# A two-block mixer kernel: scores between gate quarters, PSUM banks of the decays, an output gate by seven half-block products

## The reference

```
z = h @ w_in                      # 512 tokens, and 256 context tokens before them
# first mixer (gated linear attention), 4 heads in 2 pairs, 2 directions, chunks of 64:
dec = exp(where(causal, b[t] - b[s], -inf))            # b: sums of log decays
att = einsum('bhtd,bhsd,bhtsd->bhts', q, k, dec)       # the "scores"
o   = (q * exp(b)) @ S + att @ v                       # S: running state
S   = S * exp(b_last) + (k * exp(b_last - b)).T @ v
# second mixer (gated delta rule): a 3x3 convolution per channel over a grid of 8 x 64
qkv = silu(conv_grid(concat(bq, bk, bv), gdn_conv))    # 1536 channels
bq, bk = l2norm(bq) * 128 ** -0.5, l2norm(bk)
# ... the chunked delta rule ...
ya = rmsnorm(oa) * silu(ag)       # ag = h @ w_in[:, AG], 512 columns
yb = rmsnorm(ob) * silu(bg)       # bg = h @ w_in[:, BG], 512 columns: the output gate
```

## Time and profile before

| | |
|---|---|
| median of 3 runs | 1341.34 us (1338.7 to 1341.41) |
| profiled execution | 1342.3 us, its span 1340.5 us |
| mean granted TensorE clock | 0.995 of full |
| PE, PEld busy | 1291.7 us (96%), 795.4 us (59%) |
| DVE, ACT, POOL busy | 694.0 us (52%), 413.0 us (31%), 396.9 us (30%) |

### The profile page before, as it was taken

The page is one execution under the profiler, slowest core; times in us unless marked ns, Lnnn a source line. Parts: engine busy times, 40 slices in busy tenths (PEclk is TensorE's granted clock), DMA queues, the critical chain, the costliest instruction groups (busy, mean ns, idle before and its releaser), DMA issues.

```text
span 1340.5 us, 23888 instructions
## 1 busy us (share of the span) xinstructions
PE 1291.7 (96%) x9603; PEld 795.4 (59%) x9603; DVE 694.0 (52%) x1422; ACT 413.0 (31%) x897; POOL 396.9 (30%) x470
## 2 busy tenths in 40 slices
PE   5999999999999999999999999998999999998997
PEld 3554655555666777778445786445655786445653
DVE  4366657846333434464465374237736383337735
ACT  4244303362432222201014102236623202236721
POOL 0100000211324443154530250127731150127731
PEclk9999899999999999999999999999999999999999
DMA  9710112101310100031254415110002515100001
GB/s 315 269 63 27 39 64 78 62 1 64 119 73 3 65 2 3 3 126 64 87 192 95 133 32 188 64 52 1 2 16 67 153 41 188 63 1 2 1 1 63
DMA packets 71533, 96.54 MB, mean 72 GB/s; under 512 B 27640, under 2 KB 35248, under 8 KB 71423
## 3 DMA queue, kind: packets, MB, share of 16 engines
q1 hardware_dynamic: 71050, 94.76, 21.1%
q10 hardware_dynamic: 372, 0.27, 0.1%
HBM read 92.89 MB, written 2.13 MB: 71 GB/s over the span
## 4 chain that ended last, share of the span: by engine, by line
PE 89%; DVE 4%; POOL 2%; ACT 2%; issue 1%; DMA 1%; ACTq 0%; SPq 0%; POOLq 0%; DVEq 0%
PE PS L147 85%; PE PS L2785 2%; DVE AR L2891 1%; ACT AR L3013 1%; POOL AR L3072 1%; DMA AR<-in_onehot 1%; DMA AR<-in_final_g 1%; POOL AR L2008 1%; PE PS L353 0%; POOL AR L3070 0%; DVE AR L2878 0%; ACT AR L3023 0%; PE PS L2119 0%; DVE AR L2061 0%; PE PS L1395 0%
## 5 line engine op out<-in xcount | busy, mean ns | idle before, releaser
L147 PE MATMUL PS<-AR 64*64 64x64 f32 (+14 forms) x8966 | 1218.8, 332 | 22.4 <-ACT AR L3023 6.5
L147 PEld LDWEIGHTS PS<-AR 128*128 128x128 f32 (+4 forms) x8966 | 725.4, 155 | 488.2 <-issue 392.0
L3013 ACT ACTIVATE AR<-AR 128x257 f32<-128x257 f32 (+5 forms) x160 | 84.9, 531 | 98.4 <-DVE AR L2891 89.0
L2891 DVE CUSTOM_DVE_ANT_0 AR<-PS,AR 128x257 f32<-128x257 f32 (+5 forms) x160 | 72.3, 452 | 60.7 <-PE PS L147 43.1
L412 POOL TENSOR_TENSOR AR<-AR 128x1 f32<-128x1 f32 (+4 forms) x26 | 21.9, 843 | 260.4 <-DVE AR L407 213.7
L1183 DVE SCALAR_TENSOR_TENSOR AR<-AR 128x441 f32<-128x441 f32 (+2 forms) x96 | 78.6, 819 | 15.7 <-ACT AR L1140 12.0
L1570 DVE TENSOR_TENSOR AR<-PS,AR 128x256 f32<-128x256 f32 x60 | 25.5, 425 | 100.7 <-PE PS L147 97.6
L3072 POOL TENSOR_SCALAR AR<-AR 128x257 f32<-128x257 f32 (+5 forms) x96 | 53.8, 560 | 58.5 <-DVE AR L2897 51.0
L3070 POOL TENSOR_SCALAR AR<-AR 128x128 f32<-128x128 f32 (+3 forms) x64 | 39.2, 613 | 63.1 <-DVE AR L2897 58.2
L1697 ACT ACTIVATE AR<-PS 128x512 f32<-128x512 f32 x48 | 28.7, 597 | 92.5 <-PE PS L147 90.1
L2008 POOL TENSOR_TENSOR AR<-AR 128x512 f32<-128x512 f32 x36 | 47.7, 1326 | 28.2 <-DMA AR<-in_w_o 25.2
(11 more groups left out here) (264 smaller groups left out, 941.8 us busy)
## 6 DMA issues: line engine op xcount, KB each, us to landing
AR<-in_w_in SPq DMA_DIRECT2D x16, 2048.0 KB, 8.9
AR<-in_w_mod SPq DMA_DIRECT2D x6, 2048.0 KB, 12.7
AR<-in_w_out SPq DMA_DIRECT2D x4, 2048.0 KB, 12.6
AR<-in_x SPq DMA_DIRECT2D x8, 512.0 KB, 5.6
AR<-in_w_in SPq DMA_DIRECT2D x4, 1024.0 KB, 7.4
AR<-in_w_o SPq DMA_DIRECT2D x2, 2048.0 KB, 7.8
AR<-in_w_in SPq DMA_DIRECT2D x2, 1664.0 KB, 8.7
AR<-in_w_in SPq DMA_DIRECT2D x12, 256.0 KB, 4.2
```

What stands on the lines that cost most here:

```text
L147: return t.matmul(o, l, r, start=s, stop=p, skip_group_check=True)
L2891: v.do.tensor_tensor_reduce(PB[j % NJP][e][:, 0:nk], ps["s", l, j, e][:, 0:nk], bias_for(qb, kind, 2 * a + e, nk), 1.0, 3e38, ALU.add, ALU ...
L3013: a_.do.activation(P, P, ACT.Exp, bias=mn[:, j % NJS, e:e + 1], scale=-1.0, accum_out=su[:, j % NJS, e:e + 1]).then_inc(sa, na("p", l, j, e))
```

## The change

Three edits.

1. First mixer: the first pair's scores are put between the quarters of gate tile 1, as the second pair's stand between those of tile 3; gate tile 2 comes after the second pair's state sums; the second pair's key transposes stand between the quarters of gate tile 0, all four in bank 7. Gate tiles use banks 6 and 7, scores banks 0 to 3, output tiles banks 4, 6, 0, 4 (two each). ACT's order follows: it copies gate tiles 0 and 1, evicts the first pair's first output tile, makes two key exponentials, evicts three output tiles, makes the other six exponentials, and then passes the gates through silu.
2. Second mixer's output gate: for each half of its 512 columns, a 2 x 2 block product by seven block products instead of eight, each of 4 products of 128x128 by 256 columns. POOL makes the sums of the weight blocks after the squares, DVE those of the token blocks after group 7's taps, DVE adds the products out of PSUM after its last taps, and ACT's silu reads SBUF. PE enters the delta stage when DVE has finished its taps and not its last additions.
3. Delta stage: banks 4 and 5 leave the ring of the first 18 tiles, which has five banks then.

```diff
         gla_sums_t(t, 0)
-        gate_tile(0)
-        gla_ends_t(t, 1, (7, 0, 1, 2))
-        for a in range(4):
-            gla_scores_t(t, 0, a, (6, 0))
-        gla_out_t(t, 0, (2, 4))
-        gla_sums_t(t, 1)
-        gate_tile(1)
-        gate_tile(2)
-        for a in range(4):
-            gate_tile(3, 2 * a, 2 * a + 2)
-            gla_scores_t(t, 1, a, (6, 2))
-        nt.mark("weights", 3)
-        gla_out_t(t, 1, (4, 0))
+        for i in range(4):
+            gate_tile(0, 2 * i, 2 * i + 2)
+            gla_ends_t(t, 1, i, 7)
+        for hp in range(2):
+            if hp:
+                gla_sums_t(t, 1)
+                gate_tile(2)
+            for a in range(4):
+                gate_tile(1 + 2 * hp, 2 * a, 2 * a + 2)
+                gla_scores_t(t, hp, a, (0, 2))
+            if hp:
+                nt.mark("weights", 3)
+            gla_out_t(t, hp, (4, 6, 0, 4))
...
-        a_.wait_ge(st, nt["ag", 0])
-        a_.do.activation(gate[0], ps["ag", 0][:, :], ACT.Copy, bias=0.0, scale=1.0).then_inc(sa, na("ag0"))
-        ps.empty(sa, na, "ag", 0)
         for n in range(2):
             gla_ends_a(a_, 1, n, exp=False)
-        gla_out_a(a_, 0)
-        gla_keys_a(a_, 1)
-        a_.do.activation(gate[0], gate[0], ACT.Silu, bias=0.0, scale=1.0).then_inc(sa, na("ag", 0))
+        for a in range(2):
+            a_.wait_ge(st, nt["ag", a])
+            a_.do.activation(gate[a], ps["ag", a][:, :], ACT.Copy, bias=0.0, scale=1.0).then_inc(sa, na())
+            ps.empty(sa, na, "ag", a)
+        gla_out_a(a_, 0, 0)
+        gla_keys_a(a_, 1, 0, 2)
         for a in range(1, 4):
+            gla_out_a(a_, 0, a)
+        gla_keys_a(a_, 1, 2, 8)
+        for a in range(2):
+            a_.do.activation(gate[a], gate[a], ACT.Silu, bias=0.0, scale=1.0).then_inc(sa, na("ag", a))
+        for a in range(2, 4):
...
+    SHARED = ((1, 2), (6, 7), (5, 3), (4,))
+    NEED_S, NEED_T = {5: 1, 6: 2, 7: 3, 3: 4}, {5: 1, 6: 2, 7: 3, 4: 4}
...
+    def sums_of_rows_b(v):
+        for i, o, x, y in ((1, T1b, bf_, be_), (2, T2b, bh_, T1b), (3, T3b, bh_, bf_), (4, T4b, bg_, T2b)):
+            v.do.tensor_tensor(o, x, y, ALU.subtract).then_inc(sv, nv("bT", i))
+
+    def sums_of_weights_b(g, p):
+        w, = weights(g, 7)
+        a, b, c, d = bg_blocks(w, p)
+        s1, s2, s4_ = SB[p]
+        for i, o, x, y, op in ((1, s1, c, d, ALU.add), (2, s2, s1, a, ALU.subtract), (3, c, a, c, ALU.subtract), (4, s4_, b, s2, ALU.subtract)):
+            g.do.tensor_tensor(o, x, y, op).then_inc(sg, ng("bS", p, i))
+
+    def seven_bg_t(t, p, w):
+        a, b, c, d = bg_blocks(w, p)
+        s1, s2, s4_ = SB[p]
+        for k in range(4):
+            o = ps.take(t, "b7", p, k)
+            for i, what in enumerate(SHARED[k]):
+                if what in NEED_S:
+                    t.wait_ge(sg, ng["bS", p, NEED_S[what]])
+                if what in NEED_T:
+                    t.wait_ge(sv, nv["bT", NEED_T[what]])
+                left, right = {1: (a, be_), 2: (b, bg_), 3: (s4_, bh_), 4: (d, T4b), 5: (s1, T1b), 6: (s2, T2b), 7: (c, T3b)}[what]
+                for q in range(4):
+                    x = mm(t.go, o[:, 256 * i:256 * i + 256], left[:, q, :], right[:, q, :], q == 0, q == 3)
+            x.then_inc(st, nt("b7", p, k))
+
+    def seven_bg_v(v, p):
...
+        v.wait_ge(sa, na["g1b", p])
+        sum_of(A[:, 0:256], 0, 1, g1)
+        ps.empty(sv, nv, "b7", p, 0)
+        sum_of(u2, 1, 0, g1)
+        sum_of(u3, 1, 1, u2)
+        ps.empty(sv, nv, "b7", p, 1)
+        sum_of(B[:, 256:512], 2, 0, u3)
+        sum_of(u2, 2, 0, u2)
+        sum_of(A[:, 256:512], 2, 1, u2, "bg", 2 * p)
+        ps.empty(sv, nv, "b7", p, 2)
+        sum_of(B[:, 0:256], 3, 0, u3, "bg", 2 * p + 1)
+        ps.empty(sv, nv, "b7", p, 3)
...
         w, = weights(t, 7)
-        for h in range(4):
-            if h % 2 == 0:
-                decay_sums(t, h // 2)
-            p = ps.take(t, "bg", h)
-            projT(t, p, w, 128 * h, 128, 256, 768, ("bg", h))
+        for p in range(2):
+            decay_sums(t, p)
+            ps.ring = [b for b in range(8) if b != ps.of["gam",]]
+            seven_bg_t(t, p, w)
...
+        for p in range(2):
+            a.wait_ge(st, nt["b7", p, 0])
+            a.do.activation(G1b[p], ps["b7", p, 0][:, 0:256], ACT.Copy, bias=0.0, scale=1.0).then_inc(sa, na("g1b", p))
         for h in range(4):
-            a.wait_ge(st, nt["bg", h])
-            a.do.activation(gateB[h], ps["bg", h][:, :], ACT.Silu, bias=0.0, scale=1.0).then_inc(sa, na("bg", h))
-            ps.empty(sa, na, "bg", h)
+            a.wait_ge(sv, nv["bg", h])
+            a.do.activation(gateB[h], gateB[h], ACT.Silu, bias=0.0, scale=1.0).then_inc(sa, na("bg", h))
...
+            if m == 7:
+                sums_of_rows_b(v)
+        nv.mark("inputs", "delta")
+        for p in range(2):
+            seven_bg_v(v, p)
         nv.mark("at", "conv")
...
+        for p in range(2):
+            sums_of_weights_b(g, p)
         for k, (xv, sc) in enumerate(segs):
...
-        t.wait_ge(sv, nv["at", "conv"])
+        t.wait_ge(sv, nv["inputs", "delta"])
...
-        ps.ring = [b for b in range(8) if b != ps.of["gam",]]
+        ps.ring = [b for b in range(8) if b not in (4, 5, ps.of["gam",])]
```

More of the change, by code:

```diff
@@ L639, in gla_t @@
             if a == 2:
-                gla_ends_t(t, 0)
+                for i in range(4):
+                    gla_ends_t(t, 0, i)
         nt.mark("weights", 2)
@@ L644, in gate_tile @@
         def gate_tile(a, lo=0, hi=8):
-            p = ps.banks[(6, 6, 7, 0)[a]] if lo else ps.take(t, "ag", a, bank=(6, 6, 7, 0)[a])
+            p = ps.banks[6 + a % 2] if lo else ps.take(t, "ag", a, bank=6 + a % 2)
             for t8 in range(lo, hi):
@@ L651, in gla_t, with gla_ends_t @@
         gla_sums_t(t, 0)
-        gate_tile(0)
-        gla_ends_t(t, 1, (7, 0, 1, 2))
-        for a in range(4):
-            gla_scores_t(t, 0, a, (6, 0))
-        gla_out_t(t, 0, (2, 4))
-        gla_sums_t(t, 1)
-        gate_tile(1)
-        gate_tile(2)
-        for a in range(4):
-            gate_tile(3, 2 * a, 2 * a + 2)
-            gla_scores_t(t, 1, a, (6, 2))
-        nt.mark("weights", 3)
-        gla_out_t(t, 1, (4, 0))
+        for i in range(4):
+            gate_tile(0, 2 * i, 2 * i + 2)
[10 more added lines that the diff above has]
+            gla_out_t(t, hp, (4, 6, 0, 4))
         ps.ring = list(range(8))
         nt.mark("at", "gla")
[L668 to L675, removed]
+    def gla_ends_t(t, hp, i, bank=None):
+        n, a0, a1 = i // 2, 4 * (i % 2), 4 + 2 * (i % 2)
+        t.wait_ge(sv, nv["kd", hp, n])
+        p = ps.take(t, "kn", hp, n, a0, bank=bank)
+        for a in range(a0, a1):
+            x = t.go.transpose(p[:, 128 * (a - a0):128 * (a - a0) + 128], E[:, n, 128 * a:128 * a + 128], ident)
+        x.then_inc(st, nt("kn", hp, n, a0))
     def sums_at(n, step):
@@ L726, in gla_out_t @@
             t.wait_ge(sv, nv["s", hp])
-            p = ps.take_two(t, "oa", hp, a, bank=banks[a % 2]).rearrange("p (h x) -> p h x", h=2)
+            p = ps.take_two(t, "oa", hp, a, bank=banks[a]).rearrange("p (h x) -> p h x", h=2)
             for n in range(2):
@@ L943, in gla_a @@
             ps.empty(sa, na, "ag", a)
-        gla_out_a(a_, 1)
+        for a in range(4):
+            gla_out_a(a_, 1, a)
         na.mark("at", "gla")
@@ L953, in gla_queries_a, with gla_keys_a @@
             a_.do.activation(x2, U[:, q, 256:768], ACT.Exp, bias=0.0, scale=1.0 / 16).then_inc(sa, na("qx2", q))
[L955 to L960, removed]
+    def gla_keys_a(a_, hp, i0=0, i1=8):
+        for i in range(i0, i1):
+            n, j = i // 4, i % 4
+            reg, s0, s1 = key_region(hp, n, j)
+            a_.wait_ge(sv, nv["key", hp, n, j])
+            a_.do.activation(reg, reg, ACT.Exp, bias=0.0, scale=1.0 / 16).then_inc(sa, na("key", hp, n, j))
     def gla_ends_a(a_, hp, n, exp):
@@ L973, in gla_ends_a, with gla_out_a @@
             ps.empty(sa, na, "kn", hp, n, a0)
[L975 to L981, removed]
+    def gla_out_a(a_, hp, a):
+        a_.wait_ge(st, nt["oa", hp, a])
+        a_.do.activation(oA[:, a, 256 * hp:256 * hp + 256].rearrange("p (h n) -> p h n", h=2),
+                         ps.two("oa", hp, a).rearrange("p (h n) -> p h n", h=2)[:, :, 0:128],
+                         ACT.Copy, bias=0.0, scale=1.0).then_inc(sa, na())
+        ps.empty(sa, na, "oa", hp, a)
     def gla_g(g):
@@ L1076, in program @@
     sqs = [Cv(64 * x_.shape[1]) for x_, _ in segs]
+    BT_at = Cv.b
+    T1b, T2b, T3b, T4b = (AR[:, BT_at + 1024 * i:BT_at + 1024 * i + 1024].rearrange("p (k n) -> p k n", k=4) for i in range(4))
+    SB = [[AR[:, BT_at + 4096 + 512 * (3 * p + i):BT_at + 4608 + 512 * (3 * p + i)].rearrange("p (k n) -> p k n", k=4) for i in range(3)]
+          for p in range(2)]
+    assert BT_at + 7168 <= TOT - 2048
+    oBf = oB.rearrange("p a n -> p (a n)")
```

(2 more changed lines are left out.)

9 lines of the change are left out of this document (added).

## The result

| | median | runs | against before |
|---|---|---|---|
| before | 1341.06 us | 1338.04 to 1341.51, 9 | |
| after | 1344.15 us | 1342.71 to 1345.0, 9 | 1.0027 [1.0018, 1.0035] |

Slower: by the ratio 0.27%, which is 3.6 us. The median lies above the range of the forecast (1335.5 to 1343.7). The profiled execution of after took 1344.37 us for a span of 1342.6, 2.07 more than that of before.

What follows compares the result with a forecast made beforehand. PE, busy 96% of the span, was taken to bound the kernel. The terms -2.4 - 3.4 + 4.2 + 0.85 + 0.2 = -0.55 us, set against the median 1341.34, gave 1340.8 us; range 1335.5 to 1343.7.

Steps and rivals of the forecast that it cites:

- Edit 1: First mixer's tail: scores between gate quarters remove a wait and the half clock; -2.4 us, from -3.2 to -1.5.
- 6.7 us at half lose 3.35 us of PE's work: First mixer's tail: edit 1 removes the half clock seen from 146.9 to 153.6 us, regaining 3.35 us.
- The wait for DVE's states: First mixer's tail: second pair's scores wait for DVE's state operations to free bank 1; 1.1 us, bounds 0 and 1.7.
- Edit 2, products: Output gate: 56 products of 256 columns take 24.1 us instead of 27.5; -3.4 us on PE.
- Edit 2, collision: Convolution stage: POOL's weight sums beside group 8's taps stretch them to 12.0 us; PE waits +4.2 us, bounds 0 and 6.4.
- The slack: Between DVE's group 8 and PE's ninth norm tile: 2.65 us at ACT plus 1.9 at PE absorb lateness.
- Rival 1: No costly collision: POOL's sums slow the taps by less than 4 us or run before them; 1335.7 us, chance 0.33.
- The third rival: Full exclusion of DVE and POOL at group 8: taps take 14.2 us; 1343.0 us, chance 0.08.
- Behind the wait: After PE's wait at the ninth norm tile: later banks come free in time, no further cost booked.
- The clock behind the wait: After PE's wait at the norm tiles: a possible clock fall, bounds 0 and 3.35 us, a quarter taken, +0.85.
- rival 4: PE's wait at the norm tiles lets the clock fall for 6.7 us at half; slower, 1344.3 us, chance 0.09.
- Edit 3: Delta stage's start: waits of 1.55 us in the five-bank ring for 1.32; +0.2 us, from -1.3 to +1.5.

Runs made afterwards that it cites:

- weights_in_gap: Changed kernel with only POOL's weight sums put behind group 8's taps, DVE's row sums staying ahead of them: 1336.83 us, ratio 0.9978 to before.
- rows_in_gap: Changed kernel with only DVE's row sums put behind group 8's taps, POOL's weight sums unmoved: 1338.06 us, ratio 0.9988 to before.
- filled_again: Changed kernel with ten unread 256-column products behind the eighth norm tile, second measurement of that program: 1344.7 us, ratio 1.0036 to before.
- seven_only: Edit 2 alone on the kernel before: 1347.48 us, ratio 1.0063.
- gap_seven_banks: Changed kernel with row sums and weight sums both behind group 8's taps and edit 3 undone: 1340.37 us, ratio 1.0005 to before.
- filled_wait: Changed kernel with ten unread 256-column products behind the eighth norm tile, first measurement: 1346.8 us, ratio 1.0056 to before.
- no_scores: Edits 2 and 3 together on the kernel before, without edit 1: 1345.54 us, ratio 1.0034.

## Why the prediction was wrong

**What bounds the kernel: right.** What the profiles show of the difference was a wait of PE, its work, or its clock.

**Edit 1: the waits right, the main gain wrong.** Predicted -2.4, in the profiled pair -1.95, in the median about 0. The step that failed first is "Removed: ... 6.7 us at half lose 3.35 us of PE's work". Rows 3 are one execution, and the fall does not come in every one: of four profiles with the old order one has it in full, one by half, two not at all. In full it costs 3.0 us (8.99 for 5.96), not 3.35. That the pair of profiles came so near the forecast is luck: the trace I had read was one with the full fall. The wait for DVE's states was predicted at 1.1 and is 0.89; for bank 7 I took 0.5, it is 0.47. The second pair's state sums were said to begin after ACT's last output tile "as now"; they wait 0.76 for 0.56. And my terms gave -3.2 + 1.1 = -2.1: the -2.4 has 0.3 in it for which only "rounding of the queue delays" stands, and no row.

**Edit 2, products: right.** -3.4 predicted. From the tail's end to the rounds weights_in_gap takes 163.76 us and before 166.79; with edit 3's +0.3 taken out that is -3.3.

**Edit 2, collision: right.** Row sums 5.9 predicted, 5.73 measured; eight taps 12.0 and 11.85; the wait 4.2 and 4.73. The 0.5 us more is DVE's: the short taps behind the collision took 1.89 us instead of 1.00, beside the last weight sums. So group 8 ends 9.3 us late instead of 8.7, reckoned from the tail's end, and less the slack of 2.65 + 1.9 that makes 4.75. The slack, read from before, held. weights_in_gap shows the other side of it: no such overlap, no wait. Rival 1 said that the sums might slow the taps by less than 4 us; they slow them by 5.9.

The third rival was full exclusion, by the Trainium skill (SBUF — State Buffer, "Who interferes with whom"). The taps would then take 14.2 us; the trace has 11.85. The 14.2 was priced with a square of POOL (1.04 us); the weight sums themselves take 1.30 with DVE idle (10.36 us for eight in weights_in_gap), so one whole instruction after the other would make 8 x (1.30 + 0.75) = 16.4 us. Beside each other the eight taps take 11.85 us and the eight sums 12.46. So the two engines do lose to each other, DVE nearly twice its time and POOL a fifth of its own, but by less than full exclusion. The page's rule agrees with the trace on which operations meet, and is too dear in its size here.

**Behind the wait: a term put at nothing.** "Afterwards DVE and ACT are late by 6 us and PE by 4.2, which leaves the later banks free in time." It does not: PE's ninth norm tile starts as soon as the first logarithm is done, and the short tiles behind it wait a little for the next ones. At the full clock this costs 0.7 us, the same in rows_in_gap and in filled_again.

**The clock behind the wait: the step that failed second.** "A fall like the first costs 3.35; bounds 0 and 3.35, and I take a quarter, +0.85." In the profile of after it cost 1.74, and it fell in four executions of four, at 1.0 to 2.6. The 4.2 us was known to lie between a wait without a fall and one with, and a quarter was a guess on the cheap side; half the bound would have been right. The prediction had named a fall behind this wait as a sign that it is wrong, and that sign came. It is rival 4's mechanism, at half its price.

**Edit 3: right.** +0.2 predicted, +0.31 measured (1.39 + 0.24 for 1.32). What my sum could not show is that it is worth 3.4 us beside edit 2: the sum priced it with edit 2's delay already in the waits, and so without knowing that the old ring would have cost 3.54.

**The sum.** For the profiled pair, by measured terms: -1.95 (tail) - 3.3 (products) + 4.73 (wait) + 1.74 (clock) + 0.31 (edit 3) = +1.53, and with the 0.7 of small waits behind the wait +2.2; +1.93 + 0.26 = 2.19 was found. For the median, edit 1 is 0 instead of -1.95, which gives +4.2; the ratios 1.0027 and 1.0032 are 3.6 and 4.3 us. Against the forecast of -0.55: 2.4 from edit 1, 0.9 from the clock, 0.5 from the wait, 0.7 from the small waits, 0.2 from edit 3 and the products.

The chances: 0.17 for slower was too little. Rival 4 needed a fall of the clock behind the wait, and the wait was longer than one after which the clock had fallen. And 0.33 for rival 1 was too much: L1207's row, which I had written against it myself, was the same collision.

## What to carry to other kernels

Before you book a gain for a clock fall that a profile shows, ask whether it comes in every execution: the spread of the runs tells (before 1337.7 to 1342.5, the kernel without the fragile place 1339.2 to 1340.2), or a second profile. When work moves to VectorE or GpSimd "for free", ask not how long it is but what runs beside it on the other of the two; here one moved line on POOL was worth 7 us of the changed kernel's time. And a long PE wait costs more than its length: here four waits of 4.7 us cost 1.0 to 2.6 us of clock behind them, and 0.7 us more where the banks then came free one by one.

## What the runs showed of the hardware

- The clock fell in some executions and not in others at the same place of the same instructions: behind thin products and waits of 1.29 and 1.34 us it was half for 6.8 and 3.4 us, behind 1.31 and 0.87 us not at all. With waits of 4.7 us it fell every time (four of four), after 2.4 to 4.6 us of standing still. With waits of 3.54 us it fell both times: in seven_only 2.4 us into the wait, in gap_seven_banks 0.8 us after PE had begun again. The 32 records behind them took 3.68 and 3.44 us for 1.97. In waits of 2.61 and 2.68 us (filled_wait, filled_again) it did not fall.
- The falls listed here lasted 3.4 us or 6.8 us; no other length was seen.
- Eight taps of VectorE (128x441) and eight sums of GpSimd (128x512) take 5.98 and 10.36 us apart, 11.85 and 12.46 beside each other.
- One instruction load of 0.02 MB fell among SP's issues, one issue took 1.54 us there (median 0.43), and 13 us later PE waited 2.3 us longer than in no_scores. In filled_wait the same: 1.31 us for one issue, a wait of 2.61. That the load is the cause is argued from these two against twelve without.
